# Two-layer hybrid encoder trunk: the layer loop written out with one weight ring, the last projection computed with tokens on partitions, and merge gates ordered one unit ahead of the mixes

## What is computed

```python
h = rmsnorm(x, norm_g[l])
proj = h @ w_in[l]          # 1024 -> q, k, v, gates, mixer inputs (4864 columns), then merge, 3*1024
out_a = sliding_window_attention(rope(a_q), rope(a_k), a_v, sinks[l]) * silu(a_gate)
out_b = spatial_gating(gelu(b_u), gelu(b_v), sp_w[l], sp_b[l], ...) * silu(b_gate)
out_c = rmsnorm(hgrn2_chunkwise(c_q, 1 - f, c_i, log(f)), ...) * silu(c_gate)
gates = sigmoid(merge.reshape(b, s, 3, D) + b_merge[l])
mixed = einsum('bsnc,ncd->bsnd', stack([out_a, out_b, out_c]), w_branch[l])
y = sum(gates * mixed, axis=2) @ w_out[l]
x = x + y
# after both layers:
return rmsnorm(x, final_g)
```

## Time and profile before

| | |
|---|---|
| runs | 1055.05, 1055.41, 1055.82 us |
| the profiled execution's own time | 1055.07 us |
| its span (first to last instruction) | 1053.3 us |
| mean granted TensorE clock | 0.988 |
| TensorE (PE) busy | 1021.1 us, 97% |
| VectorE (DVE) busy | 648.6 us, 62% |
| ScalarE (ACT) busy | 528.6 us, 50% |
| GpSimd (POOL) busy | 311.5 us, 30% |

### The profile page before, as it was taken

How to read it: one execution, slowest core, us unless ns; L and a number is a source line. 1 busy time by engine, 2 the same in 40 slices (tenths; PEclk the granted TensorE clock), 3 DMA queues, 4 the chain that set the end, 5 groups by cost and what they waited for, 6 DMA issues and landing times.

```text
span 1053.3 us, 15662 instructions
## 1 busy us (share of the span) xinstructions
PE 1021.1 (97%) x6397; PEld 858.6 (82%) x6397; DVE 648.6 (62%) x847; ACT 528.6 (50%) x802; POOL 311.5 (30%) x160
## 2 busy tenths in 40 slices
PE   4899999999999999999999999999999999999996
PEld 3689899888788888888887889988888888888885
DVE  5877994599554453544638689359964354453655
ACT  5667665787552232222447666469745232232333
POOL 3331111542432332323212111055143142322422
PEclk8899999999999999999999999999999999999998
DMA  6242222212132332323333222122212332322424
GB/s 194 70 132 73 78 82 81 67 55 82 61 100 80 101 100 92 108 80 120 110 104 120 81 81 80 43 80 81 81 60 61 100 120 80 100 89 94 138 81 159
DMA packets 98540, 97.41 MB, mean 92 GB/s; under 512 B 2320, under 2 KB 96736, under 8 KB 98464
## 3 DMA queue, kind: packets, MB, share of 16 engines
q1 hardware_dynamic: 98256, 96.06, 29.4%
q0 software_dynamic: 80, 0.26, 0.1%
q10 hardware_dynamic: 128, 0.04, 0.0%
HBM read 94.26 MB, written 2.10 MB: 91 GB/s over the span
## 4 chain that ended last, share of the span: by engine, by line
PE 81%; DVE 12%; issue 3%; ACT 2%; DMA 1%; DVEq 0%; POOL 0%; ACTq 0%; POOLq 0%
PE pj L419 25%; PE pj L421 24%; PE pj L420 24%; DVE level_ops L1289 2%; PE mx L548 1%; DVE decay L1277 1%; DVE attnT L1329 1%; DVE sum_sq L1105 1%; PE mx L511 1%; DVE level_ops L1292 1%; PE mx L488 1%; PE mx L576 1%; PE mx L496 1%; DVE gate L1154 1%; DMA pos_int<-in_positions 1%
## 5 line engine op out<-in xcount | busy, mean ns | idle before, releaser
L963 POOL TENSOR_TENSOR w_lo<-w_raw,w_hi 128x1024 fp32r<-128x1024 f32 (+1 forms) x98 | 211.1, 2154 | 602.7 <-ACT w_hi L728 550.6
L419 PE MATMUL pj<-h_hi,w_hi 128*128 128x512 f32 x832 | 330.5, 397 | 1.6 <-issue 1.6
L420 PE MATMUL pj<-h_lo,w_hi 128*128 128x512 f32 x832 | 324.9, 390 | 0.0
L421 PE MATMUL pj<-h_hi,w_lo 128*128 128x512 f32 x832 | 324.8, 390 | 0.0
L728 ACT ACTIVATE w_hi<-w_raw 128x1024 fp32r<-128x1024 f32 (+1 forms) x184 | 160.5, 922 | 166.1 <-PE pj L421 164.4
L1187 DVE TENSOR_TENSOR w_lo<-w_raw,w_hi 128x1024 fp32r<-128x1024 f32 (+1 forms) x92 | 159.0, 1728 | 58.5 <-ACT w_hi L728 58.2
L419 PEld LDWEIGHTS pj<-h_hi,w_hi 128*128 128x128 f32 x832 | 156.8, 188 | 37.2 <-issue 5.1
L421 PEld LDWEIGHTS pj<-h_hi,w_lo 128*128 128x128 f32 x832 | 156.7, 188 | 33.1
L420 PEld LDWEIGHTS pj<-h_lo,w_hi 128*128 128x128 f32 x832 | 156.9, 189 | 32.2 <-issue 1.0
L1158 DVE TENSOR_TENSOR merge_gate<-pj,rstd 128x512 f32<-128x512 f32 x48 | 33.2, 691 | 164.6 <-PE pj L421 164.6
L784 ACT ACTIVATE merge_gate<-merge_gate,small 128x512 f32<-128x512 f32 x48 | 34.3, 715 | 99.5 <-DVE merge_gate L1158 99.4
(11 more groups left out here) (221 smaller groups left out, 1525.5 us busy)
## 6 DMA issues: line engine op xcount, KB each, us to landing
w_raw<-in_w_in SPq DMA_DIRECT2D x62, 1024.0 KB, 5.5
w_raw<-in_w_branch SPq DMA_DIRECT2D x24, 512.0 KB, 3.4
w_raw<-in_w_out SPq DMA_DIRECT2D x8, 1024.0 KB, 5.0
w_raw<-in_w_in SPq DMA_DIRECT2D x5, 512.0 KB, 4.5
x_tokens<-in_x SPq DMA_DIRECT2D x4, 512.0 KB, 9.0
out<-out_tokens SPq DMA_DIRECT2D x8, 256.0 KB, 2.6
sp_w_rows<-in_sp_w SPq DMA_DIRECT2D x2, 512.0 KB, 3.9
ln_g<-in_sp_ln_g SPq DMA_DIRECT2D x2, 256.0 KB, 4.3
```

What stands on the lines that cost most here:

```text
L419: pe.matmul(bank, wh, ah, start=first, stop=False)
L420: pe.matmul(bank, wh, al, start=False, stop=False)
L421: return pe.matmul(bank, wl, ah, start=False, stop=final)
L963: return pool.tensor_tensor(out=dst, in0=full, in1=hi.bitcast(f32), op=ALU.subtract)
```

## The change

- **Loop.** Both layers are written out. Semaphores are no longer cleared: they count on through both layers, and waits ask for the layer's base plus the old count (`counted`, `upto`). `layer_go` and `layer_done` are gone. Units are numbered 0 to 95 through both layers, and one ring of three `w_raw` buffers serves them all.
- **Order.** `merge` 0, `merge` 1, `mix` 0, `merge` 2, `mix` 1, ... `merge` 11, `mix` 10, `mix` 11: a gate is projected one unit ahead of the mix before it.
- **The last output projection.** In the second layer y is the stationary operand and `w_out` moves, so that the result has tokens on partitions. The whole of `w_out` is split on chip: `w_out_hi0`/`w_out_lo0` hold its first 512 columns (out units 92 and 93 of the ring) over the old `h_hi`/`h_lo`, `w_out_hi1`/`w_out_lo1` the other 512 over `branch_hi`/`branch_lo`. Unit 92 (`LAST_OUT`) is loaded to a buffer of its own, `w_raw_last`. Eight groups of 24 matmuls (j = 0 to 7, j = 0 and 1 interleaved) write eight banks, four token blocks for each half of the columns.
- **x back to tokens.** Eight hooks of four transposes (`x_to_tokens`), at every third job from 44 on in the second layer, turn `xT` back to tokens, and ACT copies them back in place (`x_back`).
- **The end.** For each bank DVE adds x, ACT squares with a running sum; after the second half of a token block ACT takes `Ln` and `Exp` of the mean square and scales the low half, DVE scales the high half, and SP sends both.

```diff
-         + [(k, p * 3 + n) for p in range(4) for n in range(3) for k in ("merge", "mix")]
+         + [(k, i - (k == "mix")) for i in range(13) for k in ("merge", "mix") if 0 <= i - (k == "mix") < 12]
...
+LAST_OUT = 2 * NU - 4
+X_BACK = 44
...
+        WOH = [at(f"w_out_hi{h}", [P, KT, T], r, f32r) for h, r in enumerate((r_hh, r_brh))]
+        WOL = [at(f"w_out_lo{h}", [P, KT, T], r, f32r) for h, r in enumerate((r_hh + 16 * KB, r_brl))]
...
+        def counted(layer):
+            return lambda s, v: layer * per_layer[s.num] + v
...
+            for v in range(RB, DEPTH * NU):
+                if v == LAST_OUT:
+                    sp.wait_ge(state_ready, counted(1)(state_ready, 2))
+                else:
+                    before = max(w for w in range(v) if slot(w) == slot(v))
+                    if before < LAST_OUT:
+                        sp.wait_ge(pj_done, jobs_to(before))
...
+                load_weights(sp, v)
...
+                def x_to_tokens(j):
+                    half, tb = divmod(j, TB)
...
+                    for c in range(4):
+                        last = pe.transpose(M[j % 2][:, c * P:(c + 1) * P],
+                                            XT[:, 4 * half + c, tb * P:(tb + 1) * P], ID)
+                    last.then_inc(xk_done, 1)
...
+                def out_tokens():
+                    for j in range(2 * TB):
+                        half, tb = divmod(j, TB)
...
+                        if j % TB == 0:
+                            pe.wait_ge(w_lo, LAST_OUT + 2 * half + 2)
+                            pe.wait_ge(w_lo_vec, LAST_OUT + 2 * half + 2)
...
+                            last = three(out_bank(j)[:, :], YH[:, k, rows], YL[:, k, rows], WOH[j // TB][:, k, :],
+                                         WOL[j // TB][:, k, :], k == 0, k == KT - 1)
...
+                        if j == 0:
+                            for k in range(KT):
+                                pe.wait_ge(y_lo, upto(y_lo, k + 1))
+                                add_y(0, k)
+                                add_y(1, k)
...
-            with pe.Fori(0, DEPTH) as layer:
...
+            for layer in range(DEPTH):
+                program(layer)
...
+                def out_stats(j):
+                    half, tb = divmod(j, TB)
+                    act.wait_ge(o_sum, j + 1)
+                    chained(act.activation(SQD[:, :], (OUTH if half else OUTL)[:, tb, :], ACT.Square,
+                                           accum_out=(SQH if half else SQL)[:, tb:tb + 1]))
...
+                    chained(act.activation(RO[:, tb:tb + 1], SQH[:, tb:tb + 1], ACT.Ln, bias=SQB[:, tb:tb + 1],
+                                           scale=1.0 / D))
+                    act.activation(RO[:, tb:tb + 1], RO[:, tb:tb + 1], ACT.Exp, scale=-0.5).then_inc(o_rstd, 1)
...
+                    act.activation(OUTL[:, tb, :], OUTL[:, tb, :], ACT.Copy, scale=RO[:, tb:tb + 1]).then_inc(o_low, 1)
...
+                for n in range(NJ + 4):
+                    if n < NJ and JOBS[n][1] == 0 and 1 < layer * NU + JOBS[n][0] + 1 < DEPTH * NU:
+                        split_lo(layer * NU + JOBS[n][0] + 1)
...
+                    dve.scalar_tensor_tensor(out=dst, in0=dst, scalar=RO[:, tb:tb + 1],
+                                             in1=FGB[:, T:D], op0=ALU.mult, op1=ALU.mult).then_inc(o_high, 1)
```

More of the change, by code:

```diff
@@ new lines, in level @@
+                def level(p, lev):
+                    s = 64 >> lev
+                    pe.wait_ge(ops_ready, upto(ops_ready, LEVELS * p + lev + 1))
+                    ops = XL[lev % 2]
+                    bank = M[3 + lev % 2]
+                    if lev == 0:
+                        for hb in range(2 * TB):
+                            low, up = (ops[:, hb * P + u * 64:hb * P + u * 64 + 64] for u in range(2))
+                            rows = slice(hb % 2 * 64, hb % 2 * 64 + 64)
+                            last = pe.matmul(bank[rows, hb // 2 * 64:hb // 2 * 64 + 64], low, up, start=True, stop=True)
+                        last.then_inc(lev_done, 1)
+                        return
+                    pe.wait_ge(at_evac, upto(at_evac, (LEVELS + 1) * p + lev))
+                    for hb in range(2 * TB):
@@ new lines, in state_updates @@
+                def state_updates(p):
+                    pe.wait_ge(khT_evac, upto(khT_evac, p + 1))
+                    evacuated(pe, FIRST[("ci", p)] + 1, layer)
+                    for hh in range(2):
+                        h = 2 * p + hh
+                        for c in range(3):
+                            last = pe.matmul(M[3 + hh][:, c * P:(c + 1) * P], KHT[:, hh, c, :],
+                                             VC[:, c, h * P:(h + 1) * P], start=True, stop=True)
+                    last.then_inc(upd_done, 1)
@@ new lines, in spatial @@
+                def spatial(ct):
+                    if ct == 0:
+                        pe.wait_ge(wT_ready, upto(wT_ready, 1))
+                        pe.wait_ge(gv_ready, upto(gv_ready, 1))
+                        pe.wait_ge(oa_evac, upto(oa_evac, 4))
+                    if ct == 3:
+                        pe.wait_ge(gated, upto(gated, SG_JOBS.index(FIRST[("bu", 0)]) + 1))
+                    bank = M[ct % 3]
+                    for nb in range(TB):
+                        for g in range(2):
+                            c = (2 * ct + g) * HD
+                            last = pe.matmul(bank[g * HD:(g + 1) * HD, nb * P:(nb + 1) * P], GV[:, nb, c:c + HD],
+                                             WT[:, 2 * ct + g, :], start=True, stop=True)
+                    last.then_inc(sv_done, 1)
@@ new lines, in program @@
+                for p, d in enumerate(DIAG):
+                    hooks[d].append((diagonal, p))
+                    for lev in range(LEVELS):
+                        hooks[d + 1 + lev].append((level, p, lev))
+                    for step, f in enumerate((transpose_khat, state_updates, recurrent_out, head_norm)):
+                        hooks[d + 1 + LEVELS + step].append((f, p))
+                hooks[20].append((transpose_spatial,))
+                for ct in range(4):
+                    hooks[(25, 26, 27, 29)[ct]].append((spatial, ct))
@@ L630, in _ @@
                 for n in range(NJ):
+                    if n == FIRST[("out", 0)] and layer == DEPTH - 1:
+                        out_tokens()
+                        break
                     if n in (0, FIRST[("out", 0)]):
@@ L718, in rsqrt @@
                 return act.activation(dst, dst, ACT.Exp, scale=-0.5)
-            def split_hi(u, layer):
-                if u < RB:
-                    act.wait_ge(first_in[u], 16 * (layer + 1))
-                else:
-                    act.wait_ge(raw_in[u % RB], loaded(u))
-                if u >= WB:
-                    act.wait_ge(pj_done, JOBS_TO[u - WB])
-                for half in range(2):
-                    act.activation(part(WHI[:, u % WB, :], u, half), part(RAW[:, u % RB, :], u, half), ACT.Copy)\
-                       .then_inc(w_hi, 1)
@@ L1023, in _ @@
-                pool.drain()
-                pool.wait_ge(layer_done, 4)
-                pool.sem_clear(range(first_num, last_num + 1))
-                pool.sem_inc(layer_go, 1)
-            pool.wait_ge(fg_in, 16)
-            for i, n in enumerate(E_POOL):
-                half, tb = divmod(n, TB)
-                c = slice(half * T, (half + 1) * T)
-                pool.wait_ge(e_scaled, i + 1)
-                pool.tensor_tensor(out=OUT[:, tb, c], in0=OUT[:, tb, c], in1=FGB[:, c], op=ALU.mult)\
-                    .then_inc(e_evac_pool, 1)
+            for layer in range(DEPTH):
+                program(layer)
```

1699 lines of the change are left out of this document (855 added, 844 removed).

## The result

The changed kernel takes 1057.99 us (median of 12 runs, 1057.27 to 1058.66), the kernel before in the same comparison 1055.74 us (12 runs, 1054.88 to 1056.44). The ratio is 1.0023, 95% interval [1.0014, 1.0032]. The profiled execution after took 1057.98 us, with a span of 1056.2: 2.9 more than before on either measure.

The account below looks back on a forecast made before the run. PE, busy 97% of the span, was taken to bound the kernel, with time gained only where it stands still. Terms 0 + 0 + 3.2 + 3.3 + 1.5 + 0 - 5.9 = +2.1 on 1055.07 gave 1057.2 us; range 1052.8 to 1060.4.

Parts of the forecast that it names:

- line for "slower": Whole kernel: a time above 1057.5 us counts as slower, about 0.2% being indistinguishable from no change; chance of slower 0.41.
- signs of being wrong: No gap at the last projection, clock at 1.00 after a gap over 3 us, or a tail not about 6 us shorter.
- The loop written out: Both layers: writing out the loop leaves the late matmul at the second layer's start; 0, ends -1.9 and +1.5 us.
- second layer starts clean: Rival: the 1.87 us between starts at 562 goes with the loop, giving 1055.3 us; chance 0.14.
- Gates a unit ahead: Merge and mix stretch: the new order moves no work onto or off PE; 0, ends +0.3 and -0.3 us.
- Transposes: Second layer's stream: 32 transposes of x in eight hooks cost PE +3.2 us, ends 3.0 and 4.4.
- The wait: Before the last projection: PE waits for POOL's second-unit half until 3.6 us after mix 11's end (M); net +3.3 us.
- a longer wait: Rival: DVE reaches mix 11's first sum as late as before; wait 5.6, clock 2.2, time 1059.9 us; chance 0.20.
- no wait: Rival: at the last projection POOL's order doesn't hold PE and the clock stays up; 1052.1 us, chance 0.15.
- The clock: Behind the wait before the last projection the granted clock falls; +1.5 us, ends 0 and 2.2.
- The last projection's matmuls: Last output projection: 192 matmuls of 512 columns as before, second half's weights hidden; 0.
- The tail: From the last out matmul's start (L) to the span's end: 9.4 us instead of 15.3; -5.9, ends -6.7 and -5.1.

Follow-up runs that it names:

- e1: Changed kernel with POOL making its half of the second out unit right behind the first unit's, before `y_lo` of block 6; 1053.75 us.
- e2: Changed kernel with 14 additional useless matmuls filling PE's wait in front of the first y matmul of the last projection; 1056.76 us.
- e9: As e7, with DVE also making its half of the first cf unit's weights ahead of the third rotary step; 1056.15 us.
- e4: Changed kernel with merge and mix in the old order and the last two `w_out` units' splits at the last mix; 1060.15 us.
- e10: As e1, with DVE making its half of the second out unit before the gated sum of mix 11's first job; 1052.56 us.
- e7: Changed kernel with DVE making its half of the v unit's weights between q's two rotary steps, one job earlier, in both layers; 1060.34 us.
- e3: Changed kernel without the eight hooks of transposes and ACT's copies of x back, so the output is not the layer's; 1054.52 us.
- e6: Changed kernel with `Sqrt` on ACT and a reciprocal on DVE in place of `Ln` and `Exp` in the last norm; 1056.26 us.
- e11: Edits of e10, e9 and e6 together, plus 17 useless matmuls before PE's first wait for the first layer's sum of squares; 1044.99 us.

## Why the prediction was right, step by step

The forecast was 1057.2 us, the result is 1057.99, inside the range. In the profiled executions it was +2.1 against +2.9. The forecast lay just below the prediction's own line for "slower" (1057.5) and the result lies just above it, a case to which it had given a chance of 0.41. None of its signs of being wrong was seen. By its steps:

- **The loop written out, 0.** Right. The trace after is 0.3 late already before 104 us (103.37 and 103.66, the same matmul), in the stretch where the start's half clock ends a little sooner or later, and stays there. It is no price of the loop that the traces could show: at the first layer's last mix matmul (489.12 in before) kernels whose edits leave the first layer's program as it is in the changed kernel stand from 0.6 earlier (e1) to 0.6 later (e2). The reading of the earlier trace rows held as well: the late matmul at the second layer's start remained, and e9 took it away by DVE's order alone. The rival "second layer starts clean" has fallen.
- **Gates a unit ahead, 0.** Right for the stream (e4: 229.68 and 229.67), with +0.29 at the first layer's step, the end of my range. What I had put under another step is the order's real effect: with the old one, and the splits where that one has them, the wait is 5.84 us.
- **Transposes, +3.2.** Measured +3.9 (0.121 each, not 0.100). I priced by a hook of eight; the changes of kind around a hook of four weigh more. Inside my ends, and the largest of the misses: 0.7 of 0.8 us.
- **The wait, M + 3.6.** Measured M + 4.03. The chain was the predicted one, link by link: POOL's half of the second unit, behind `y_lo`. DVE began the product of mix 11's first job (995.89) 0.26 us after the job's end, which I had not counted. POOL's split took 2.79 beside DVE instead of 2.40, and `y_lo` 1.51 instead of 1.74. Net +3.7 for +3.3. e1 is the proof: two POOL instructions exchanged, 4.2 us with the clock. What the rival "a longer wait" hung on, ACT's split of the second out unit, ended at 994.78, M - 3.6, near the M - 3.9 of my count. The rival "no wait" (1052.1) is e10's kernel, at 1052.56.
- **The clock, +1.5.** Measured +1.45, and e2 shows the cause. But I was lucky in the size: behind a wait of 4.03 (4.02 in e9) the same stretch cost 1.39 (e7), 1.45, 1.50 (e3), 1.68 (e9) and 2.58 us (e6) over 43.41, and 2.32 behind e4's 5.84. The upper end of 2.2 was too low. The Trainium skill, "TensorE: Matmul & The Clock Gate", section "HAM oscillation", says that waits between bursts make the next burst start cold; the runs agree (0.50 behind 4.03 and 2.82 us). Its remedies are a loop restructured so that PE stays warm or padding; e2 and e11 keep PE busy with useless work instead.
- **The last projection's matmuls, 0.** 43.41 us in both layouts (994.44 to 1037.85; e10: 998.30 to 1041.71).
- **The tail, L + 9.4, -5.9.** Measured L + 8.96, -6.5 by the timelines' starts (0.17 of the miss is the chain's start in the earlier trace rows, later than the timeline's). Two misses met inside it: the last output is issued at L + 6.2, not at L + 6.0, and from there to the end are 2.7 us, not 3.4. I also had only half of the reason for the saving: half of it comes from the next layer's splits, which I had not seen in before's chain.

The sum of errors is 0.7 + 0.4 + 0.3 (start) - 0.6 = +0.8. The steps missed in both directions; the result is nearer than they were. That it came so near is in part luck. "Faster" would have needed another order on POOL; e1 is that kernel.

## What to carry to other kernels

When a change makes one consumer need two producers' results at once, look at what stands between the two in the producer's own order: here one `y_lo` that nobody wanted for another 8 us cost 4.2 us. Before you move a step off the path on a busy engine, follow the next two consumers as well, since a stall that is removed comes back at the one whose producer was pushed (e7), and may be longer there and cost clock as well. And where a wait can't go, filling it with useless matmuls keeps the clock: 1.2 and 2.9 us here.

## What the runs showed of the hardware

- Waits of 1.5 us (562 in the changed kernel, 997 in e1) left the granted clock at 1.00; one of 2.82 and those of 4.03 and 5.84 brought it to 0.50.
- How long the clock stays down behind one and the same wait varies: 1.39 to 2.58 us were lost in the last projection with identical code there (five kernels, one execution each). A kernel with such a wait has an uncertainty of about 1 us in one profiled execution that it would not have without.
- A DVE operation with two operands in on-chip memory that starts beside a POOL subtraction ends about when POOL has ended and its own length is over: 565.08 + 2.85 = 567.93, and POOL's end is 567.39. The Trainium skill, "SBUF — State Buffer", section "SBUF: two separate sides", calls the port that the two share an exclusive lock, held for the whole instruction; that agrees here, where POOL had come first (567.39 and 0.54 more, of a usual 0.68), as does `product`, which reads a PSUM bank (998.55 in the changed kernel, beside `y_lo`) and kept its 0.69.
- `Sqrt`, `Square` and scaled copies follow one another on ACT without a table load in the last three token blocks of e6 (the first has one, at 1033.91), while in the changed kernel `Ln` and `Exp` cost one of 1.28 us each, in every block.
